# A transformer block in float32: dense products as one float32 product each, in place of three split ones, and the memory keys and values computed inside the front block

## The reference

```python
h = rms_norm(x, ffn1_pre_g)
x = x + 0.5 * rms_norm(swiglu(h, w_gate, w_up, w_down), ffn1_post_g)   # D_FF = 2816
h = rms_norm(x, mix_pre_g)
proj = h @ w_in                                  # then shifted blends on the rwkv part
o_nsa = nsa_mixer(...)                           # compressed, selected and window attention
o_rwkv = rwkv7_mixer(...)                        # a recurrence over the tokens
mixed = concat([rms_norm(o_nsa), o_rwkv]) @ w_out
x = x + rms_norm(mixed, mix_post_g)
h = rms_norm(x, mem_pre_g); m = rms_norm(mem, mem_kv_g)        # mem: 256 tokens
x = x + rms_norm(memory_cross_attention(h, m, wq, wk, wv, wo), mem_post_g)
# and a second swiglu block like the first
```

## Time and profile before

| | |
|---|---|
| median of three runs | 3118.57 us (3118.14 to 3120.81) |
| the profiled execution, its own time | 3117.75 us |
| its span in the trace | 3116.0 us |
| PE busy | 2847.9 us (91%), 19800 matmul records |
| PEld busy | 2329.8 us (75%) |
| DVE busy | 1420.3 us (46%) |
| ACT busy | 891.6 us (29%) |
| POOL busy | 137.9 us (4%) |
| mean granted clock of PE | 0.952 of full speed |

### The profile page before, as it was taken

How to read it: one execution, slowest core, us unless ns; L and a number is a source line. 1 busy time by engine, 2 the same in 40 slices (tenths; PEclk the granted TensorE clock), 3 DMA queues, 4 the chain that set the end, 5 groups by cost and what they waited for, 6 DMA issues and landing times. The chain is left out here.

```text
span 3116.0 us, 47363 instructions
## 1 busy us (share of the span) xinstructions
PE 2847.9 (91%) x19800; PEld 2329.8 (75%) x19800; DVE 1420.3 (46%) x2624; ACT 891.6 (29%) x1695; POOL 137.9 (4%) x138
## 2 busy tenths in 40 slices
PE   5999999998499997669999999699987999999995
PEld 4888888887377776658888887577776888888884
DVE  4333333342634353247877776653443333343335
ACT  4121121211433332224444444342432111121111
POOL 0000000000200000011111111000000000000002
PEclk9999999999589998879999999799998999999997
DMA  4112111110422254351111100540122211112103
GB/s 143 41 40 67 40 54 40 40 40 37 133 80 88 77 178 153 121 131 47 39 33 33 33 19 8 197 142 1 52 84 82 67 40 54 40 40 67 40 13 114
DMA packets 200492, 214.26 MB, mean 69 GB/s; under 512 B 61588, under 2 KB 172435, under 8 KB 200340
## 3 DMA queue, kind: packets, MB, share of 16 engines
q1 hardware_dynamic: 200340, 212.11, 21.8%
HBM read 165.84 MB, written 40.99 MB: 66 GB/s over the span
## 5 line engine op out<-in xcount | busy, mean ns | idle before, releaser
L343 DVE TENSOR_TENSOR f_prod<-f_up_ps,f_silu 128x512 f32<-128x512 f32 x88 | 60.8, 691 | 763.3 <-ACT f_silu L307 763.3
L307 ACT ACTIVATE f_silu<-f_gate_ps 128x512 f32<-128x512 f32 x88 | 52.6, 598 | 1082.4 <-PE f_up_ps L380 1082.4
L1681 PE MATMUL fr_dense_ps<-one_hi,fr_wh 128*128 128x512 f32 x400 | 170.6, 426 | 11.4 <-DVE fr_wl L1898 11.4
L1682 PE MATMUL fr_dense_ps<-one_lo,fr_wh 128*128 128x512 f32 x400 | 159.8, 399 | 0.0
L1683 PE MATMUL fr_dense_ps<-one_hi,fr_wl 128*128 128x512 f32 x400 | 159.5, 399 | 0.0
L358 DVE TENSOR_TENSOR ffn_y<-f_down_ps,ffn_y 128x512 f32<-128x512 f32 x176 | 116.8, 687 | 57.7 <-PE f_down_ps L396 57.7
L358 DVE TENSOR_TENSOR y<-f_down_ps,y 128x512 f32<-128x512 f32 x176 | 116.8, 687 | 57.7 <-PE f_down_ps L396 57.7
L2345 PE MATMUL mt_d_ps<-mt_wh,two_hi 128*128 128x512 f32 x256 | 108.7, 425 | 33.0 <-DVE two_lo L2535 24.5
L395 PE MATMUL f_down_ps<-f_d1l,f_a1h 128*128 128x512 f32 x352 | 136.9, 389 | 0.0
L394 PE MATMUL f_down_ps<-f_d0h,f_a0h 128*128 128x512 f32 x352 | 136.9, 389 | 0.0
L396 PE MATMUL f_down_ps<-f_d0h,f_a0l 128*128 128x512 f32 x352 | 136.9, 389 | 0.0
(11 more groups left out here) (399 smaller groups left out, 7207.0 us busy)
## 6 DMA issues: line engine op xcount, KB each, us to landing
f_rawg<-in_ffn_w_gate SPq DMA_DIRECT2D x22, 1024.0 KB, 5.4
f_rawu<-in_ffn_w_up SPq DMA_DIRECT2D x22, 1024.0 KB, 7.9
fr_raw<-in_w_in SPq DMA_DIRECT2D x25, 512.0 KB, 4.2
f_rawd<-in_ffn_w_down SPq DMA_DIRECT2D x11, 1024.0 KB, 4.9
arena<-in_ffn_w_down SPq DMA_DIRECT2D x11, 1024.0 KB, 5.0
arena<-x SPq DMA_DIRECT2D x16, 512.0 KB, 4.3
x<-arena SPq DMA_DIRECT2D x16, 512.0 KB, 2.7
n_x<-in_x SPq DMA_DIRECT2D x8, 512.0 KB, 4.3
```

What stands on the lines that cost most here:

```text
L307: nc.scalar.activation(silu[:, h, :], gate_ps[:, h, :], ACT.Silu).then_inc(silu_done[h], 1)
L343: nc.vector.tensor_tensor(prod[:, h, :], up_ps[:, h, :], silu[:, h, :], ALU.mult).then_inc(prod_done[h], 1)
L1681: nc.tensor.matmul(dense_ps[:, b, cols], w_hi[:, b, k, :], hi[:, k, cols], start=(k == 0), stop=False)
L1682: nc.tensor.matmul(dense_ps[:, b, cols], w_hi[:, b, k, :], lo[:, k, cols], start=False, stop=False)
```

## The change

- Every dense product is one `matmul` call on plain float32 tiles: the `hi` and `lo` tiles, the casts on ACT and the subtractions on DVE are gone, in both FFNs, the front, the memory products, the tail and the copies after the turns.
- The FFN loops are written out, with the weights of two pairs in SBUF (`w`, `wd`); the first pair copies into `y` in place of adding to zeros, so POOL's memset goes.
- `renorm`'s residual add moves from POOL to DVE.
- The memory stages go. Their 8 key chunks and 8 value chunks follow the 25 chunks of the front block (`CHUNKS` is 41); the norm of the memory tokens is done on the way (`msq`, `mxn`, `mturn`, `mhi`). The front's weights have four buffers in place of two.
- `load_masks` goes; the masks and the small constants of "ar" are loaded from ACT's queue as that stage starts, and no longer behind the keys in SP's queue.
- The tail keeps two sets of weights in SBUF, its mixed operand is written straight into `two_x`, and the planner's costs are new: half a chunk of the front (8 calls) 3.5, a product of the tail 0.44, a pair of `L2391` calls 0.95 where it was 1.75.

```diff
 def hidden(i, j, h):
-    pe.wait_ge(gu_lo, i * 4 + 2 * j + 2)
-    pe.wait_ge(prod_done[h], i * 2 + j)
+    if i or j:
+        pe.wait_ge(prod_done[h], i * 2 + j)
     for k in range(KD):
         for ps, n in ((gate_ps, 0), (up_ps, 1)):
-            nc.tensor.matmul(ps[:, h, :], w_hi[j][n][:, k, :], hi[:, k, at], start=(k == 0), stop=False)
-            nc.tensor.matmul(ps[:, h, :], w_hi[j][n][:, k, :], lo[:, k, at], start=False, stop=False)
-            mm = nc.tensor.matmul(ps[:, h, :], w_lo[j][n][:, k, :], hi[:, k, at],
-                                  start=False, stop=(k == KD - 1))
+            mm = nc.tensor.matmul(ps[:, h, :], w[:, i % 2, n, k, j * P:(j + 1) * P], x[:, k, half(h)], start=(k == 0), stop=(k == KD - 1))
...
 # renorm, DVE
+                    dve.wait_ge(x_in_sems[t % BUFS], 16 * (t // BUFS + 1))
+                    dve.wait_ge(scaled, t + 1)
+                    nc.vector.tensor_tensor(x[:, t % BUFS, :], x[:, t % BUFS, :], y[:, t, :], ALU.add).then_inc(added, 1)
...
 # the front block's planner and PE
-        event(("mm", c, 0), "pe", 5.5, ("w_lo", c), ...)
+        event(("mm", c, 0), "pe", 3.5, ("load", c), ...)
...
+            def mem_product(c):
+                pe.wait_ge(w_in[c % 4], 16 * (c // 4 + 1))
+                pe.wait_ge(evacuated, c - 1)
+                if c == PROJECTED:
+                    pe.wait_ge(wide_read, use_of(("mturn", 0)) + 1)
+                    pe.wait_ge(mem_copied, 2)
...
+                    for k in range(KD):
+                        mm = nc.tensor.matmul(out, w[:, c % 4, k, :], x[:, k, rows], start=(k == 0), stop=(k == KD - 1))
...
+                        for k in range(KD):
+                            mm = nc.tensor.matmul(out, x[:, k, rows], w[:, c % 4, k, :], start=(k == 0), stop=(k == KD - 1))
...
 # attend_and_recur, ACT, ahead of its plan
+            for dst, name in ((m_gram, "m_gram"), (m_low, "m_low"), (m_one, "m_one"), (m_lev, "m_lev"), (eye, "eye"),
+                              (mean_pair, "mean_pair"), (mean_all, "mean_all")):
+                act.dma_start(dst[:], a[name]).then_inc(masks_in, 16)
...
 # memory_tail
-                for x_, (lhsT, at, rhs, to) in enumerate(terms):
-                    mm = nc.tensor.matmul(dense_ps[b][:], lhsT[:, k, at], rhs[:, k, to], start=(k == 0 and x_ == 0),
-                                          stop=(k == KD - 1 and x_ == 2))
+                mm = nc.tensor.matmul(dense_ps[b][:], lhsT, rhs, start=(k == 0), stop=(k == KD - 1))
```

More of the change, by code:

```diff
@@ L103, in renorm @@
 def renorm(core, tag, x_in, tiles, consts, y=None, post_gain=None, factor=1.0, x_out=None,
-           pre_gain=None, hi=None, lo=None):
+           pre_gain=None, turned_to=None):
     nc = core.nc
     ident, eps = consts["ident"], consts["eps"]
-    add, turn = y is not None, hi is not None
+    add, turn = y is not None, turned_to is not None
     BUFS = 4
@@ L193, in _ @@
                     act.wait_ge(turned, t + 1)
-                    for h in range(2):
-                        nc.scalar.copy(hi[:, 4 * h:4 * h + 4, t * P:(t + 1) * P], tp[:, t % 2 * 2 + h]).then_inc(hi_done, 1)
+                    nc.scalar.copy(turned_to[:, :, t * P:(t + 1) * P].rearrange("p (h k) t -> p h k t", h=2), tp[:, t % 2 * 2:t % 2 * 2 + 2]).then_inc(copied, 1)
         @block.vector
@@ L204, in _ @@
             dve.wait_ge(gains_in, 16 * (add + turn))
-            for step in range(tiles + 2):
+            for step in range(tiles + 1):
                 t = step
@@ L218, in _ @@
                                                    in1=g_pre[:], op0=ALU.mult, op1=ALU.mult).then_inc(normed, 1)
[L219 to L233, removed]
         if turn:
@@ L558, in load_masks @@
-def load_masks(core, ctx, a):
-    nc = core.nc
-    shapes = {"causal": [P, T], "window": [P, 5 * P], "cmp": [P, TT, 63], "row_ok": [P, 1]}
-    masks = {n: sbuf(nc, ctx, f"{n}_mask", s) for n, s in shapes.items()}
-    loaded = core.sem("masks_loaded")
-    with nc.Block() as block:
-        @block.sync
-        def _(sp):
-            for name, tile in masks.items():
-                sp.dma_start(tile[:], a[f"mask_{name}"]).then_inc(loaded, 16)
-            sp.wait_ge(loaded, 16 * len(masks))
-    return masks
@@ L1340, in front_chunks @@
         cols.append(chunk * P)
+    for kind in ("memk", "memv"):
+        for n in range(KD):
+            kinds.append((kind, n))
+            cols.append(n * P)
     return kinds, cols
@@ L1428, in front_plan @@
             event(("store_v", n), "sp", 0.2, ("tcopy", n), late=4.0)
+    event(("load_mem",), "sp", 0.5, ("store_ops", 3), ("store_bonus", 3), late=5.0)
+    for t in range(2):
+        event(("msq", t), "act", 1.9, ("load_mem",), t and ("msq", 0))
+        event(("mxn", t), "dve", 1.5, ("msq", t), t and ("mxn", 0))
+        event(("mturn", t), "pe", 1.0, ("mxn", t), ("cfin", 1) if t else room(("mturn", 0)), t and ("cfin", 0))
+        event(("mhi", t), "act", 1.3, ("mturn", t), ("mm", PROJECTED - 1, 0), t and ("mhi", 0))
     event(("load_w1", 0), "sp", 0.2, ("load", 3), late=7.0)
@@ L1791, in _ @@
             for e in plan:
[L1792 to L1798 removed]
+                if e[0] == "evac":
                     c = e[1]
@@ L2157, in tail_plan @@
             if st == 0:
-                after += [("mix_lo", QUARTERS - 1)] + ([("turn", 0, t - 4)] if t >= 4 else [])
+                after += [("mix_y", QUARTERS - 1)] + ([("turn", 0, t - 4)] if t >= 4 else [])
             if st == 1 and i >= 2:
```

720 lines of the change are left out of this document (243 added, 477 removed).

## The result

The changed kernel takes 3535.72 us (median of 4, 3534.87 to 3536.94); the kernel before took 3118.36 us beside it (4 runs, 3117.7 to 3120.81). The ratio is 1.1337, 95% interval [1.1317, 1.1357]: 417 us slower. The forecast was 3540 in a range of 3518 to 3572.

The account below looks back on a forecast made before the run. PE's instruction stream was taken as the bound. Terms of 370.2 (FFNs), -3.5, -11, -7, +26, -5 and +52.6 sum to +422 on 3117.75, giving 3540 us; range 3518 to 3572, held 8 in 10.

Parts of the forecast that it names:

- The price of a product: Every dense product on PE: 0.8587 us in plain float32, 0.179 us more than the three float32r matmuls it replaces.
- f1 and f2: The two FFN stages: 1056 products each, +188.6 less 3.5 for an earlier first matmul, +185.1 us each.
- rival prices of 0.880 and 0.907: Every dense product dearer than its row: 0.880 us gives 3602 us (5%), 0.907 gives 3680 us (4%).
- the plan's 0.43: Every dense product: a call is one instruction of 0.43 us, giving 2297 us, faster; chance 2%.
- Rival 2: Every dense product: four passes, each at a float32r matmul's present price, 0.907 us a product, 3680 us; chance 4%.
- r1: First renorm stage: add moved to DVE, norm 1.28 us instead of 3.46, six steady steps x 1.85, -11 us.
- r2: Last renorm stage: a tile takes 1.28 + 1.22 + 0.25 instead of 3.45 + 0.1 us, 8 x 0.8, -7 us.
- n1: First norm stage: a copy and a subtraction less at each tile's end, -3.5 us, an estimate.
- Front and memory: Front block with memory chunks: from 505.0 to 530.8 us, +26; dearer dense products against the separate memory and mask stages saved.
- ar: Attention and recurrence stage: constants from ACT's queue come some 10 us earlier, half of it taken, -5 us (0 to -10).
- mt: Tail: 384 dearer products +68.6 us, shorter chain before the first -6, no wait on split weights -8; +52.6 us.
- Rival 4: A new serial piece in the memory tokens' turns or the tail's order, 10 to 25 us, 3565 us; chance 7%.

Follow-up runs that it names:

- true prices: Changed kernel with planners told 6.9 instead of 3.5 for half a front chunk and 0.86 instead of 0.44 for a tail product: 3550.57 us.
- the second timing of the changed kernel: The changed kernel timed again unchanged, beside the follow-up runs on it: 3537.95 us.
- low prices: Split-product kernel with half a front chunk priced 3.5 instead of 5.5: 3069.43 us; later, values issued first, a tail product priced 0.44 instead of 0.68: 3053.66 us.
- the split kernel: Kernel before, float32r splits kept, the change's other parts added, the memory's 128 value products in plain float32: 3077.2 us, ratio 0.9869.

## Why the prediction was right

**The price of a product.** Right on its row: 0.8587 from 32 calls of `L2391` against 0.858 in the FFN; f1 and f2 came within 0.6 us of their terms, and the run with the FFN alone gave +370.5 for the +370.2 of the sum. The rival prices of 0.880 and 0.907 fell, and so did the plan's 0.43. Rival 2 fell by its price for a pass. The Trainium skill ("FP8 and Floating Point Precision", TensorE Precision Notes) gives four passes for true FP32, and the measured time agrees with four: 0.858 / 4 is 0.2145 us, where 512 columns at 2.4 GHz are 0.2133. What the prediction multiplied by four was the 0.2267 of a float32r matmul, which is dearer than that. So the ratio of a product to a float32r matmul is 3.8 at 512 columns (0.858 / 0.2267), 3.6 at 256 (0.432 / 0.121) and 2.0 at 128 (0.223 / 0.111): it depends on the columns, because the float32r price does not fall in step with them.

**r1, r2, n1.** r1 -12.4 for -11, r2 -6.9 for -7: the mechanism (GpSimd's add slows DVE's norm) was shown by moving the add alone, which gave -7.0 of r1 and all of r2; the rest of r1 came with the subtractions gone and was not run alone. The term for r2 was written as 8 x 0.8, which is 6.4 and not 7. n1 was mis-sized, -1.8 for -3.5. n1 is also missing where the prediction says that only "r1" and "r2" are not PE's: PE was busy 15.75 of its 35.7 us.

**Front and memory, +29.8 for +26.** The small miss hides larger ones that cancel, and that is luck. The dense part ended 460.5 us after the stage's start, where the terms make 465.0. From there to the next stage it took 74.3 us where the terms make 65.8: the value products (29.2) had the wait of 4.3 us behind the store of the keys and 3 us at the clock's lower level after it, and between the last value product at 1527.4 and the next stage's first issue at 1535.2 lay 7.8 us, where the term said 5. The step "that puts more PE work between the small products than the plan believes, so nothing should be late" was right in direction and too modest: it is worth 7 us against a plan with true prices.

**ar, +0.5 for -5.** The failed step is "I take half". The constants did come earlier and the wait for them went, 11.2 to 0.9 us, but the values, next in SP's queue, became the late ones (8.5 us): they were issued no earlier than before, and the DMA engines were busy all through (a share of 1.02 to 1.10 over the stage's first 30 us, in the second timing of the changed kernel). I had named the masks' competition and given it no price.

**mt, +37.3 for +52.6.** The largest miss; it is luck that the front's 3.8 us and ar's 5.5 offset 9 of its 15 in the total. The sign "the tail about 453 us" failed (437.3). Its listed parts make 68.6 - 6 - 8 - 1.3 = 53.3 and not 52.6. The wait ahead of the first product went from 24.5 to 18.9 us, as forecast (-6), and the one for weights went (-8). PE's idle time fell by 22.5 us in all (50 to 27.5), for a forecast of 16: the small waits for `y`, which go with a later place of the turns, weren't in the term. PE's busy time grew by 59.8 (350.0 to 409.8) for a forecast of 68.6. The term priced no clock: PE loses 4 us less to the lower level, since one of the two waits ahead of such a stretch is gone and the stretch behind the other is shorter. And it gave the plan's price no effect: with true prices PE is idle for 6.4 us more in the tail's dense stretch. So of the 15.3 us some 6.5 are waits, which true prices bring back, and 4 are the clock; the other 5, in PE's busy time, aren't attributed.

**Rival 4** (a serial piece from wrong prices, 10 to 25 us) had its sign wrong: the wrong prices were worth 12.6 us to the changed kernel, as low prices were worth 8 and 12 us to the split one. Only its first half left a trace, a wait of 1.2 us ahead of the keys, until ACT had read the turned memory tokens out of the wide buffer (`fr_wide_ps`).

## What to carry to other kernels

Price a matmul form by the starts of its own rows at its own width before swapping instruction counts: three calls became one, DVE and ACT lost 24 and 31% of their busy time (1420 to 1074 us, 892 to 614), and a product got 26% dearer on the engine that bounds the kernel. The choice goes by width: float32r splits at 512 columns (0.680 us against 0.858) and at 256 (0.36 against 0.43), plain float32 at 128 (0.223 against 0.334). Where a planner orders work for the bound engine, try a price for its long operations below the measured one: here an accurate price left that engine waiting, 4.3 us in the front and 6.4 in the tail, and a low one did not. And a change that loses can hold parts that win: try each of them on the kernel before.

## What the runs showed that I had not expected

- A float32r matmul takes 0.2267 us at 512 columns, 0.121 at 256 and 0.111 at 128, with new weights for each; a plain one 0.429, 0.216 and 0.112 an instruction, two to a product, at 512, 256 and 128. At 128 columns both kinds stand at about 0.11 us an instruction.
- A DMA issue on SP held the queue for 5 to 6.5 us (`ar_vw`, `ar_vc`) some 20 transfers into the stage, where the issues before it took 0.6 us or so each. But moving a load ahead of such issues gained only 4 us of 13, since the DMA engines were busy all through.
- True prices in a list planner made it worse, by 12.6 us of 3538, and too low ones made the split kernel better by 20 us in 3077.
- In the front PE's clock falls to the lower level while PE is never idle. In the kernel before, products of 64x128 and 1x128 run from 913.16; from 917.0 to 926.7, well into the next dense products, the clock is 0.50. Summed over slices of 1 us, PE loses 21 us to the lower level up to the last dense product of the front before the change and 20 after it. So this is not in the difference, but it is as much as the low prices gave the split kernel. The row of that stretch (length, PE's busy time, clock, DMA share, GB/s):

```profile
917.00:926.70 9.70, 9.70 (x26) 0.50 0.73 270
```
